# Padding every on-chip buffer of a three-block model kernel to begin at a multiple of 64 bytes

## The chip, the cores and the metric

The kernel runs on one core of one Trainium2 chip. The metric is the device time of that core in microseconds (us). Three runs of the kernel before gave 3527.54, 3527.82 and 3530.15 us, so the median is 3527.82 us.

## What is computed

The reference takes one sequence of 512 tokens of 1024 features through three blocks, all in 32-bit floats. Cut to what matters, a block is a few large matrix products between small stages:

```python
def first_block(x, ...):
    x = layer_norm(ALPHA * x + 0.5 * swiglu(x, w_gate, w_up, w_down), ...)   # 1024 -> 2816 -> 1024
    x = layer_norm(ALPHA * x + hybrid_mixer(x, w_in, ...), ...)   # attention and a state-space branch
    return layer_norm(ALPHA * x + 0.5 * swiglu(x, ...), ...)
```

The second block has another mixer (three branches) and a convolutional feed-forward of width 2816; the third has three branches (sparse attention, pooling, delta rule) and a feed-forward of width 4096. Every `x @ w` above is a product of 512 tokens with a weight matrix that is read from HBM once.

## The kernel before, in words

**The products.** TensorE multiplies in a reduced form of 32-bit float (`float32r`). To keep accuracy, each operand is split into a high and a low half, and each product is made of three matmuls: high with low, low with high, high with high. A weight unit of 128 partitions by 1024 floats lands by DMA in one of four buffers `ring` (line 413). ScalarE writes its high half into a buffer `w_high` (line 429), VectorE writes the rest into `w_low` (line 441). Each of the two has three buffers; some stages lend further pairs, named `f1d_place`, `o_place` and so on (`Down.place`, line 763).

**Three helpers issue nearly all large matmuls.** `tile_steps` (line 465) streams 512 tokens of the activations (`x_high`, `x_low`, or a branch's `..._yh`, `..._yl`) past 128x128 weights: 24 matmuls make one tile of 128 output features. `tensor_rows` (lines 735 to 737) and `tensor_down_tile` (lines 849 to 851) do the reverse: the weights are streamed, 512 floats wide, past 128x128 pieces of the activations (`x_high`, or small buffers `f1d_in`, `c2d_in`, `f3d_in`, `o_in`). In the trace a matmul is named `bank<-moving,stationary`: the first name is the operand that is streamed, the second the one that is loaded. Line 644 holds matmuls of 256 columns of a Strassen-like stage. The small stages use plain float32 matmuls.

**Order.** Every engine has its own hand-written program, tied by semaphores. Nothing in these programs reads an address: a buffer's place in memory sets no count, no order and no wait.

**Where buffers lie.** `Area.take` (line 151) hands out on-chip memory one buffer after the other. `self.at` counts floats per partition; the byte address is `ORIGIN + 4 * self.at`, and ORIGIN, 16512, is 258 times 64. At most FLOATS = 53200 floats are to be had. The first area (lines 232 to 246) holds what lives all through; every stage opens an area of its own behind it, at `b.base.at` or at a place inside an earlier stage. The places that follow from the sizes in the code, in floats, with what is left over when divided by 16 (16 floats are 64 bytes):

```
buffer                                     first float   over 16   bytes past a multiple of 64 / of 16
ring (4), const                            0 to 4608     0         0  / 0
cols (462 floats)                          4608          0         0  / 0
X, x_high, x_low, w_high (3), w_low (3)    5070 ...      14        56 / 8
hid, f1d_in, f2d_in, c2d_in, f3d_in        23830 ...     6         24 / 8
first block:  a_yh, a_yl (attention)       40160, 44256  0         0  / 0
first block:  z_yh, z_yl; o_in, o_place    28022 ...     6         24 / 8
second block: a_yh, g_yh, l_yh and lows    48918 ...     6         24 / 8
second block: o_place                      41756 ...     12        48 / 0
third block:  a_yh, a_yl (attention)       43068, 45116  12        48 / 0
third block:  p_yh, d_yh and lows; o_place 38950 ...     6         24 / 8
the last float taken by any buffer         53190
```

Three sizes cause it: `cols` has 462 floats (14 over 16), `cond` has 8, and in single stages 257x2, 514, 516 and 62 floats throw what follows off by another amount (and in the attention of the first block back on a multiple of 64 bytes, by five buffers of 514).

Of the kernel before, what the change touches and what calls it, by code (L numbers as in the profile page):

```python
# [16 lines left out]
FIRST = 4  # L17
ORIGIN = 16512
FLOATS = 53200
ALPHA = 2.0 ** 0.25  # L20
NEG = -1.0e30

# [122 lines left out]
class Area:  # L145
# [5 lines left out]
    def take(self, name, *shape, dtype=F32):  # L151
        n = 1
        for s in shape:
            n *= s
        assert self.at + n <= FLOATS, (name, self.at + n)
        self.b.n_tensors += 1
        t = self.b.nc.alloc_sbuf_tensor_at(f"{name}_{self.b.n_tensors}", [128, n], dtype,
                                           offset=ORIGIN + 4 * self.at, align_bytes=4)
        self.at += n
        a = t[:, :]  # L160
        if len(shape) == 2:
            return a.rearrange("p (a b) -> p a b", a=shape[0])
        if len(shape) == 3:
            return a.rearrange("p (a b c) -> p a b c", a=shape[0], b=shape[1])
        if len(shape) == 4:
            return a.rearrange("p (a b c d) -> p a b c d", a=shape[0], b=shape[1], c=shape[2])
        return a
# [1067 lines left out]
def gpsimd_ffn(b, s, ready):  # L1235
# [4 lines left out]
    for t in range(4):  # L1240
        for r in ready(t):
            gp.wait_ge(*r)
        gp.tensor_scalar(b.X[:, t, :], b.X[:, t, :], ALPHA, None, MUL).then_inc(*g.pool.up("alpha", t))

# [376 lines left out]
def gpsimd_qkv1(b, s):  # L1621
# [6 lines left out]
    for t in range(4):  # L1628
        gp.tensor_scalar(b.X[:, t, :], b.X[:, t, :], ALPHA, None, MUL).then_inc(*s.gw.pool.up("alpha", t))
    gp.wait_ge(*s.gw.pool.at("alpha", 3))  # L1630
# [3640 lines left out]
```

## Time and profile before

| | |
|---|---|
| median of three runs | 3527.82 us (3527.54 to 3530.15) |
| span of the profiled execution | 3528.6 us, clock 0.998 |
| TensorE (PE) busy | 3464.7 us, 98% |
| weight loads (PEld) | 2856.9 us, 81%, beside the matmuls |
| VectorE (DVE) | 2107.9 us, 60% |
| ScalarE (ACT) | 1497.4 us, 42% |
| GpSimd (POOL) | 333.9 us, 9% |
| DMA | 386.3 MB, 109 GB/s on average |

The profiled execution is one of its own; the page gives its span, 3528.6 us, and no other time for it. A matmul's duration in the trace is from its start to the modelled end of its results, and the next one starts long before that: durations overlap. What a matmul takes out of the span is the distance from its start to the start of the next, called its pitch here. It is read from the timeline view, where a group of equal matmuls in a row stands as one line with its count.

### The profile page before, as it was taken

How to read it: one execution, taken by the hardware profiler on the slowest of the kernel's cores; microseconds unless marked ns; L12 is line 12 of the kernel's file. 1: busy time of each engine (PE TensorE's matmuls, PEld its weight loads, DVE VectorE, ACT ScalarE, POOL GpSimd, SP SyncE). 2: the span in 40 equal slices, each digit the busy share in tenths (PEclk: the TensorE clock that was granted, in tenths of full speed). 3: DMA queues.
4: the chain of work that ended last, by engine and by line, in shares of the span. 5: the costliest groups of instructions: out<-in, count | busy, mean ns of one | idle time of the engine just before them, and what ended most of it. 6: DMA issues, size and time to landing. Idle time of an engine off the chain costs nothing. (4 is left out here: it accounts for less than half of the span.)

```text
span 3528.6 us, 45725 instructions
## 1 busy us (share of the span) xinstructions
PE 3464.7 (98%) x17532; PEld 2856.9 (81%) x17532; DVE 2107.9 (60%) x3344; ACT 1497.4 (42%) x2717; POOL 333.9 (9%) x374
## 2 busy tenths in 40 slices
PE   8999999999999999999999999999999999999999
PEld 7887888886777899887887788887787788888887
DVE  5456565678446787763344576667476567672256
ACT  2225344345443355536223363346254243452354
POOL 1000200003000100023000100000000104222100
PEclk9999999999999999999999999999999999999999
DMA  6556421220224334620322243245411320143365
GB/s 235 182 186 202 145 70 54 84 84 25 90 91 154 112 105 144 197 77 18 104 78 90 66 132 96 96 150 167 124 37 31 108 92 27 39 135 100 99 195 161
DMA packets 107974, 386.30 MB, mean 109 GB/s; under 512 B 12060, under 2 KB 14764, under 8 KB 107504
## 3 DMA queue, kind: packets, MB, share of 16 engines
q1 hardware_dynamic: 101088, 364.86, 32.0%
q0 software_dynamic: 4528, 16.43, 1.5%
q8 instruction: 142, 2.33, 0.3%
q10 hardware_dynamic: 2144, 2.10, 0.2%
q14 instruction: 72, 0.59, 0.1%
HBM read 379.13 MB, written 4.21 MB: 109 GB/s over the span
## 5 line engine op out<-in xcount | busy, mean ns | idle before, releaser
L441 DVE TENSOR_TENSOR w_low<-ring,w_high 128x1024 fp32r<-128x1024 f32 (+2 forms) x519 | 651.2, 1256 | 732.4 <-ACT w_high L429 724.5
L465 PE MATMUL bank<-x_low,w_high 128*128 128x512 f32 (+1 forms) x2144 | 839.6, 395 | 16.1 <-DVE w_low L441 9.8
L465 PE MATMUL bank<-x_high,w_low 128*128 128x512 f32 (+1 forms) x2144 | 826.6, 389 | 0.0
L429 ACT ACTIVATE w_high<-ring 128x1024 fp32r<-128x1024 f32 (+2 forms) x519 | 538.7, 1039 | 620.1 <-PE bank L465 257.5
L465 PE MATMUL bank<-x_high,w_high 128*128 128x512 f32 (+1 forms) x2144 | 542.8, 390 | 0.0
L465 PEld LDWEIGHTS bank<-x_low,w_high 128*128 128x128 f32 x2144 | 405.4, 189 | 104.6 <-issue 16.0
L465 PEld LDWEIGHTS bank<-x_high,w_low 128*128 128x128 f32 x2144 | 406.2, 189 | 84.8 <-issue 3.6
L465 PEld LDWEIGHTS bank<-x_high,w_high 128*128 128x128 f32 x2144 | 391.6, 190 | 87.8 <-issue 4.8
L735 PE MATMUL bank<-w_low,x_high 128*128 128x512 f32 (+1 forms) x384 | 147.0, 383 | 1.4 <-ACT z_z L2074 1.3
L737 PE MATMUL bank<-w_high,x_high 128*128 128x512 f32 (+1 forms) x384 | 145.6, 379 | 0.0
L736 PE MATMUL bank<-w_high,x_low 128*128 128x512 f32 (+1 forms) x384 | 145.5, 379 | 0.0
L735 PEld LDWEIGHTS bank<-w_low,x_high 128*128 128x128 f32 x384 | 72.3, 188 | 19.3 <-ACT z_z L2074 2.2
L736 PEld LDWEIGHTS bank<-w_high,x_low 128*128 128x128 f32 x384 | 72.3, 188 | 14.2 <-issue 0.2
L737 PEld LDWEIGHTS bank<-w_high,x_high 128*128 128x128 f32 x384 | 72.1, 188 | 14.3
L400 POOL DMA_DIRECT2D const<-in_consts x3 | 1.8, 588 | 862.6 <-DVE x_low L918 374.9
L3059 ACT ACTIVATE c_in<-bank 128x512 f32<-128x512 f32 x44 | 26.3, 598 | 108.6 <-PE bank L465 108.5
L4332 ACT ACTIVATE f_relu<-bank 128x512 f32<-128x512 f32 x32 | 19.2, 599 | 121.4 <-PE bank L465 121.4
L3082 DVE SCALAR_TENSOR_TENSOR c_y<-c_in,cols,c_y 128x512 f32<-128x512 f32 x88 | 66.2, 752 | 3.1
L849 PE MATMUL bank<-w_low,c2d_in 128*128 128x512 f32 x168 | 67.6, 403 | 0.0
L851 PE MATMUL bank<-w_high,c2d_in 128*128 128x512 f32 x168 | 67.4, 401 | 0.0
L850 PE MATMUL bank<-w_high,c2d_in 128*128 128x512 f32 x168 | 67.4, 401 | 0.0
L963 DVE SCALAR_TENSOR_TENSOR f_ada<-ring,cond,f_ada 128x512 f32<-128x512 f32 x84 | 65.0, 774 | 2.8
(746 smaller groups left out, 6963.9 us busy)
## 6 DMA issues: line engine op xcount, KB each, us to landing
ring<-in_W SPq DMA_DIRECT2D x686, 512.0 KB, 3.6
X<-in_x POOLq DMA_DIRECT2D x1, 2048.0 KB, 9.6
x_spill<-X POOLq DMA_DIRECT2D x1, 2048.0 KB, 8.1
X<-x_spill POOLq DMA_DIRECT2D x4, 512.0 KB, 3.6
ring<-in_W SPq DMA_DIRECT2D x4, 432.0 KB, 3.1
out<-X SPq DMA_DIRECT2D x3, 512.0 KB, 5.6
const<-in_consts POOLq DMA_DIRECT2D x1, 1133.0 KB, 11.6
f_hid<-in_xT ACTq DMA_DIRECT2D x4, 256.0 KB, 8.1
```

The source lines that it names most:

```text
L429: ac.activation(b.UH[u.place][:, 0:u.K * u.n], u.src(), ACT.Copy).then_inc(*b.split.act.up("high", i))
L441: dv.tensor_tensor(b.UL[u.place][:, 0:n], u.src(), b.UH[u.place][:, 0:n].bitcast(F32), SUB).then_inc(*b.split.dve.up("low", i))
L465: i = pe.matmul(out, w[:, k, c], v, start=n == 0 and q == 0, stop=last and q == 3 * K - 1)
L735: pe.matmul(out, xh, wl[:, q, :], start=k + q == 0, stop=False)
L736: pe.matmul(out, xl, wh[:, q, :], start=False, stop=False)
L737: i = pe.matmul(out, xh, wh[:, q, :], start=False, stop=k + q == 7)
L849: pe.matmul(out, u[:, 0, s], wl[:, 0, c], start=k == 0, stop=False)
L850: pe.matmul(out, u[:, 1, s], wh[:, 0, c], start=False, stop=False)
L851: x = pe.matmul(out, u[:, 0, s], wh[:, 0, c], start=False, stop=k == d.nk - 1)
L963: x = dv.scalar_tensor_tensor(acc, w[:, k, :], b.cond[:, 2 * q + k:2 * q + k + 1], acc, MUL, ADD)
L3059: ac.activation(s.cb[m % 3][:, 2:514], b.bk["c2u", m], ACT.Copy).then_inc(*g.act.up("copied", m))
L3082: dv.scalar_tensor_tensor(y, x[:, q:q + 512], b.col("ffn_conv_w_2", 44 * q + c), y, MUL, ADD).then_inc(*(g.dve.up("conv", m) if q == 2 els ...
```

## The change

`Area.take` rounds its position up to the next multiple of 16 floats before it places a buffer. The buffer's size, shape and content stay as they are; only first addresses move.

```diff
+LINE = 16
...
     def take(self, name, *shape, dtype=F32):
         n = 1
         for s in shape:
             n *= s
+        self.at += -self.at % LINE
         assert self.at + n <= FLOATS, (name, self.at + n)
```

The largest area ends at float 53190 before. Its padding adds 10 (2 behind `cols`, 8 behind `cond`), which makes 53200, the limit itself.

## Rows read from the trace of the kernel before

**Rows 1.** The page: busy time by engine.
```profile
PE 3464.7 (98%) x17532; PEld 2856.9 (81%) x17532; DVE 2107.9 (60%) x3344; ACT 1497.4 (42%) x2717; POOL 333.9 (9%) x374
```

**Rows 2.** Groups by form on PE (count, busy us, mean ns); lines 849 and 644 in whole.
```profile
L465 PE MATMUL bank<-x_low,w_high 128*128 128x512 f32 x1912 | 777.0, 406 | 2.0 <-issue 1.0 <-DVE w_low L441 0.7 <-DVE a_v L3398 0.2
...
L735 PE MATMUL bank<-w_low,x_high 128*128 128x512 f32 x320 | 127.8, 399 | 1.4 <-ACT z_z L2074 1.3
...
L465 PE MATMUL bank<-z_yl,w_high 128*128 128x512 f32 x128 | 52.0, 406 | 0.0
...
L465 PE MATMUL bank<-g_yl,w_high 128*128 128x512 f32 x32 | 12.7, 396 | 0.0
...
0.00:3529.00 3529.00, 390.72 (x976) 1.00 0.34 109
...
0.00:3529.00 3529.00, 162.72 (x1344) 1.00 0.34 109
```

**Rows 3.** Timeline, PE, a tile with x moving: start us, duration us, form, count.
```profile
206.95 0.39 PE L465 MATMUL bank<-x_low,w_high 128*128 128x512 f32 x1
...
212.57 0.39 PE L465 MATMUL bank<-x_low,w_high 128*128 128x512 f32 x1
```

**Rows 4.** Timeline, PE, second block, half a tile with g_y moving.
```profile
1811.13 0.40 PE L465 MATMUL bank<-g_yl,w_high 128*128 128x512 f32 x1
...
1813.95 0.39 PE L465 MATMUL bank<-g_yl,w_high 128*128 128x512 f32 x1
```

**Rows 5.** Timeline, PE, first block, a tile with a_y moving.
```profile
601.06 0.39 PE L465 MATMUL bank<-a_yl,w_high 128*128 128x512 f32 x1
...
606.63 0.39 PE L465 MATMUL bank<-a_yl,w_high 128*128 128x512 f32 x1
```

**Rows 6.** Timeline, PE, third block, half a tile with a_y moving.
```profile
2713.91 0.39 PE L465 MATMUL bank<-a_yl,w_high 128*128 128x512 f32 x1
...
2716.67 0.39 PE L465 MATMUL bank<-a_yl,w_high 128*128 128x512 f32 x1
```

**Rows 7.** Timeline, PE, a tile with z_y moving, in four pieces of 128.
```profile
1023.49 0.41 PE L465 MATMUL bank<-z_yl,w_high 128*128 128x512 f32 x1
...
1029.34 0.41 PE L465 MATMUL bank<-z_yl,w_high 128*128 128x512 f32 x1
```

**Rows 8.** Timeline, PE, 256 columns, x moving, o_place loaded: first, then second block.
```profile
1151.91 0.29 PE L465 MATMUL bank<-x_low,o_place 128*128 128x256 f32 x1
...
1154.80 0.29 PE L465 MATMUL bank<-x_low,o_place 128*128 128x256 f32 x1
...
2077.62 0.28 PE L465 MATMUL bank<-x_low,o_place 128*128 128x256 f32 x1
...
2080.50 0.29 PE L465 MATMUL bank<-x_low,w_high 128*128 128x256 f32 x1
```

**Rows 9.** Timeline, PE, o_place moving: first block to 1119.29, then second block.
```profile
1117.18 0.39 PE L849 MATMUL bank<-o_place,o_in 128*128 128x512 f32 x1
...
1119.29 0.40 PE L849 MATMUL bank<-w_low,o_in 128*128 128x512 f32 x1
...
2074.82 0.40 PE L849 MATMUL bank<-o_place,o_in 128*128 128x512 f32 x1
```

**Rows 10.** Windows, PE: length, busy (count), clock, DMA share, GB/s; c2d, then f3d.
```profile
2350.00:2410.00 60.00, 60.00 (x252) 1.00 0.57 183
...
3380.00:3500.00 120.00, 120.00 (x517) 1.00 0.61 188
```

**Rows 11.** Splits into o_place, windows 1100:1146 (first pair), 2040:2066 (second pair).
```profile
L441 DVE TENSOR_TENSOR o_place<-ring,o_place 128x1024 fp32r<-128x1024 f32 x9 | 11.0, 1222 | 1.4 <-ACT o_place L429 1.3
...
L429 ACT ACTIVATE o_place<-ring 128x1024 fp32r<-128x1024 f32 x9 | 9.4, 1046 | 0.4 <-DMA ring<-in_W 0.4
...
L441 DVE TENSOR_TENSOR o_place<-ring,o_place 128x1024 fp32r<-128x1024 f32 x6 | 7.3, 1223 | 1.1 <-ACT o_place L429 1.0
...
L429 ACT ACTIVATE o_place<-ring 128x1024 fp32r<-128x1024 f32 x6 | 6.3, 1046 | 0.0
```

## The prediction

> **What bounds the kernel now.** I read the page first: TensorE is busy 98% of the span and no other engine reaches two thirds [rows 1]. VectorE's, ScalarE's and the DMAs' work is hidden wherever TensorE streams, so a buffer's place can buy or cost time only through the matmuls themselves. The groups by form come next [rows 2]. The most frequent form streams 512 columns of x past weights: three groups of 1,912 (low with high, high with low, high with high), 5,736 matmuls. Weights streamed past x: 3 x 320 = 960. Line 849 has 976 and lines 850 and 851 the same, 2,928 in all. The streams of branch outputs follow: z_y 3 x 128 = 384; g_y, l_y, p_y, d_y and the second block's a_y 3 x 32 each, 480. With the 288 of the two other a_y these are 10,776 matmuls of 512 columns; at some 234 ns each they are 2,520 us, 71% of the span.
>
> The third view is the timeline, for the pitch, the distance from one start to the next. A tile with x moving begins at 206.95 and the next at 212.57: 5.62 us for 24 matmuls, 234.2 ns [rows 3]. Half a tile of g_y takes 2.82 us for 12, 235.0 ns [rows 4].  Here x lies 8 bytes past a multiple of 16 bytes, and so does g_y. Now the two operands that don't: the a_y of the first block begins at a multiple of 64 bytes, and its tile takes 5.57 us for 24, 232.1 ns [rows 5]; the a_y of the third block begins 48 bytes past one, which is a multiple of 16, and takes 2.76 us for 12, 230.0 ns [rows 6]. All four are loaded from the same w buffers, run through the same helper; the granted clock is 1.00 in the windows read, which is the 2.4 GHz level [rows 10]. The only thing I know that sets them apart is the first address of the moving operand. z_y is streamed as four pieces of 128, each of them 8 bytes off, and takes 5.85 us for 24, 243.8 ns [rows 7]: about 10 ns more for three more pieces, some 3 ns a piece, of the same size as the 2 to 4 ns between the one-piece cases.
>
> The loaded operand doesn't show this. 256 columns of x stream past o_place, which in the first block lies 8 bytes off 16 and in the second lies on a multiple of 16: 2.89 us for 24 (120.4 ns) against 2.88 us (120.0 ns) [rows 8]. So I put the gain to the moving operand's address, not to the loaded one's.
>
> **The change, part by part.** It adds and removes no instruction, wait or transfer. What moves is addresses. `ring` and `const` stay (they are at multiples of 64 bytes already); X, x, w and nearly every stage buffer go from 8 bytes past a 16-byte boundary to a multiple of 64. The class each stream lands in is that of rows 5, so I price with 232.1 and keep 230.0 as the good end and no gain as the bad end.
>
> - x streamed past w: 234.2 - 232.1 = 2.1 ns [rows 3, 5], times 5,736: 12.0 us. Ends: 0 and 4.2 x 5,736 = 24.1 us.
> - The 480 branch streams at 8 bytes off: 235.0 - 232.1 = 2.9 ns [rows 4, 5]: 1.4 us. Ends 0 and 5.0 x 480 = 2.4.
> - z_y, 384: nothing to 243.8 - 232.1 = 11.7 ns; whether a change of piece costs time for itself no row tells, so I take the middle, 5.9 ns: 2.3 us. Ends 0 and 5.3 (at 230.0).
> - Weights streamed past x, 960: no aligned case. Ends 0 and 4 ns; I take 1.0 ns, half of x's, because streams of weights show less in rows 9: 1.0 us, ends 0 and 3.8.
> - Weights streamed past small buffers, 2,928. o_place moving takes 2.11 us for 9 (234.4 ns) in the first block and 2.80 us for 12 (from 2074.82 to 2077.62 of rows 8; 233.3 ns) in the second, where it lies on 16 bytes [rows 8, 9]: 1.1 ns. The third block's f3d stretch has 120.00 us for 515 starts (two of the 517 were under way at the edges), 233.0 ns [rows 10], w's and places mixed. I take 1.1 ns for the third of them that stream from lent places (some 1,070) and nothing for w: 1.2 us. Ends 0 and 3 x 2,928 = 8.8.
> - 256 columns: 1,344 on line 644 [rows 2] and some 1,300 on line 465. One piece each, so the same absolute price is possible, but no aligned moving case exists. Between 0 and 2.1 ns, I take half: 1.0 x 2,640 = 2.6 us; good end 4 x 2,640 = 10.6.
> - Plain float32 matmuls, transposes: stay; their small stages wait on VectorE and ScalarE.
> - ScalarE and VectorE: writing into o_place takes ScalarE 1046 ns at either alignment and VectorE 1222 against 1223 ns [rows 11]. Nothing. The cover is TensorE's tile of 5.6 us over 2.3 us of splitting; if it fell away, an unchanged duration would still cost nothing.
> - DMA: the weights' ring doesn't move. The two 2 MB transfers of X and the spills do, outside TensorE's path.
>
> Sum: 12.0 + 1.4 + 2.3 + 1.0 + 1.2 + 2.6 = 20.5 us. From the profiled span, 3528.6 us, that is 3508.1; the median of the runs stands 0.8 below the span, so 3507.3, and I say 3507. A measurement of this kernel can tell about 0.2%, 7 us, from no change. With all good ends (24.1 + 2.4 + 5.3 + 3.8 + 8.8 + 10.6 = 55) it would be 3473.
>
> A page bears on the size. The Trainium skill, "SBUF — State Buffer", section "SBUF: two separate sides", says that on-chip memory is read in lines of 16 bytes and that a stream pays for each line it crosses into. A run of 512 floats that starts 8 bytes off touches 129 lines instead of 128; an estimate from that page is 234 / 129 = 1.8 ns, and by it the x term would be 10 us. Rows 3 and 5 agree with it.
>
> **The rivals.**
>
> *No change that can be told (25%).* What matters may be how moving and loaded operand lie to each other. x and w are both 14 over 16 floats, both 0 afterwards: their difference stays zero. In rows 5 and 6 the difference isn't a multiple of 16 bytes, and that alone could give 232.1 and 230.0. Against it stand rows 8, where the difference changes from one to the other kind and the pitch doesn't. Then x keeps 234.2, and the a_y of first and third block, which lose their odd difference, pay back 2.1 x 192 + 4.2 x 96 = 0.8 us; z_y may give 2. Time: 3526, between 3521 and 3534. The Trainium skill, "TensorE: Matmul & The Clock Gate", section "Back-to-back issue gap", is on this side: its gap for 512 columns is a function of columns and clock alone, 215.8 ns, with no address in it; the trace does not agree with its number (234.2 in rows 3), and its silence on addresses would mean 3528.
>
> *Slower (15%).* The stretch of c2d, weights streamed past c2d_in, has 60.00 us for 250 starts, 240.0 ns, where the same helper with the same alignments past f3d_in has 233.0 [rows 10]. Something in the addresses or in the phase of two streams locks c2d into a pattern that is 7 ns worse, and the same could catch other stages once everything lies at the same place within 64 bytes. Its place is any long stretch of equal matmuls; its price is about 6 ns each. It decides when more than 7 us / 6 ns = 1,170 matmuls beyond the gain are caught: with 20.5 us gained, 4,600 of them. If half of the 10,776 are caught and nothing is gained, 5,388 x 6 = 32 us: 3560. If x alone is, 3562. For it: the lock is there in the trace, unexplained. Against it: the x stream, the longest of all, shows no such pitch in rows 3.
>
> *A larger gain (12%).* The pitch goes to 230.0 or below everywhere, and c2d leaves its 240: 3473 by the good ends, with c2d's some 500 matmuls 3 us more. For it: rows 6. Against it: the operand of rows 5 is the one at a multiple of 64.
>
> That the padding doesn't take place is excluded by the arithmetic: X goes from float 5070 to 5072. It also just fits, 53190 + 10 = 53200.
>
> **How the numbers follow.** The forecast has 48%, no change 25%, slower 15%, the larger gain 12%. Faster by over 0.2%: 48 + 12 = 60%. The range reaches from 3480, which leaves out the best part of the larger gain, to 3535, which takes in all of no change and the mild part of slower; some 2 in 10 lie outside. The forecast's own range is 3495 to 3518.
>
> **What would show it.** In the changed kernel's timeline a tile of x should take 5.57 us (232.1 ns) instead of 5.62; z_y's 5.85 should fall to about 5.7; a_y of the first block should stay at 5.57; durations on ScalarE and VectorE should stay within 5 ns; TensorE's idle time should not grow. I am wrong if x stays at 234 (the rival on relative place), if a_y of the first block rises (its loaded operand's move matters), or if a stretch stands at 240.0 that did not before.

## The result and the profile after

The changed kernel takes 3469.49 us in the median of four runs (3467.41 to 3474.49), against 3528.45 us for the kernel before beside it (3527.54 to 3530.15): a ratio of 0.9835, 95% interval 0.9821 to 0.9849. It is faster by 59 us. The forecast was 3507 us with a range from 3480 to 3535: the sign was right and the size far off, on the side of the larger gain.

The page of the changed kernel, span and busy time by engine, which answers to [rows 1]:

```profile
span 3466.8 us, 45725 instructions
PE 3399.0 (98%) x17532; PEld 2838.3 (82%) x17532; DVE 2104.5 (61%) x3344; ACT 1495.5 (43%) x2717; POOL 336.3 (10%) x374
```

TensorE is busy 65.7 us less (3464.7 before), with the same 17,532 matmuls. The span falls by 61.8 us; TensorE's idle time grows from 63.9 to 67.8 us. VectorE and ScalarE stay within 4 us. So the whole difference lies in the matmuls' pitch, where the prediction had looked for it.

The timeline of the changed kernel, TensorE: a tile of x past w (to compare with [rows 3]), then a tile of a_y of the first block ([rows 5]); start, duration, form, count:

```profile
200.75 0.39 PE L467 MATMUL bank<-x_low,w_high 128*128 128x512 f32 x1
...
206.19 0.39 PE L467 MATMUL bank<-x_low,w_high 128*128 128x512 f32 x1
...
593.13 0.40 PE L467 MATMUL bank<-a_yl,w_high 128*128 128x512 f32 x1
...
598.72 0.39 PE L467 MATMUL bank<-a_yl,w_high 128*128 128x512 f32 x1
```

x takes 5.44 us for 24, 226.7 ns, where it took 5.62 us (234.2 ns). That is already below the 230.0 ns which the prediction held for the best case. a_y, at a multiple of 64 bytes before and after, takes 5.59 us (232.9 ns) against 5.57: almost the same.

A window in the middle of a long stretch of equal matmuls says the same with one line. Its columns are: window, length, TensorE's busy time, matmuls touched by it, clock, DMA share, GB/s. Two matmuls are cut by the edges, so the pitch is the length divided by the count less 2. One matmul more or less in the count is 0.4 ns in 120 us, 0.7 in 80 and 1.3 in 40, so smaller differences between windows say nothing. Four stretches of the kernel before, in this order: x past w, w past x, z_y past w, w past c2d_in:

```profile
2130.00:2250.00 120.00, 120.00 (x514) 1.00 0.29 92
1734.00:1774.00 40.00, 40.00 (x173) 1.00 0.38 119
1009.00:1089.00 80.00, 80.00 (x330) 1.00 0.37 118
2334.00:2414.00 80.00, 80.00 (x336) 1.00 0.60 192
```

The same stretches of the changed kernel, and last f3d_in, which answers to the second line of [rows 10]:

```profile
2130.00:2250.00 120.00, 120.00 (x531) 1.00 0.29 97
1702.00:1742.00 40.00, 40.00 (x178) 1.00 0.37 119
991.00:1071.00 80.00, 80.00 (x344) 1.00 0.36 118
2288.00:2368.00 80.00, 80.00 (x345) 1.00 0.60 197
3317.00:3437.00 120.00, 120.00 (x521) 1.00 0.62 191
```

Worked out: x past w from 234.4 to 226.8 ns, w past x from 233.9 to 227.3, z_y from 243.9 to 233.9, c2d from 239.5 to 233.2. The f3d stretch, w and lent places mixed, goes from 233.0 only to 231.2. Times their counts: 7.6 x 5,736 = 43.6 us, 6.6 x 960 = 6.3, 10.0 x 384 = 3.8, 6.3 x 504 = 3.2, in sum 57 of the 65.7 us. These products give all matmuls of a pair the pitch of one undisturbed stretch, so they are upper figures: added up from start to start over the two traces, waits included, x past w takes 34.9 us less, w past x 4.6, z_y 4.1 and c2d 2.6. The rest is in smaller groups. One is the stage of 256 columns (12 matmuls between the two lines), another the lent places past f1d_in (48 between the two lines). The timeline of the kernel before:

```profile
1267.48 0.65 PE L644 MATMUL bank<-f2s_sh,w_high 128*128 128x256 f32 x4
1268.93 0.65 PE L644 MATMUL bank<-f2s_sh,w_high 128*128 128x256 f32 x4
...
299.64 0.39 PE L849 MATMUL bank<-f1d_place,f1d_in 128*128 128x512 f32 x1
...
310.86 0.42 PE L849 MATMUL bank<-w_low,f1d_in 128*128 128x512 f32 x1
```

and of the changed kernel:

```profile
1262.70 0.63 PE L646 MATMUL bank<-f2s_sh,w_high 128*128 128x256 f32 x4
1264.11 0.63 PE L646 MATMUL bank<-f2s_sh,w_high 128*128 128x256 f32 x4
...
310.20 0.39 PE L851 MATMUL bank<-f1d_place,f1d_in 128*128 128x512 f32 x1
...
321.10 0.39 PE L851 MATMUL bank<-w_low,f1d_in 128*128 128x512 f32 x1
```

120.8 ns became 117.5, and 233.8 became 227.1.

What needs a cause is that buffers all at multiples of 64 bytes now run at four different pitches (226.8, 229.2, 232.9 and 233.9 ns). The table gives the first bytes modulo 256, from the sizes in the code, and the pitch of the pair. "Distance" is the loaded buffer's place less the moving one's, modulo 256. The pitches of g_y and of the two f3d rows are read like those of f1d_place, start to start over 24 to 48 equal matmuls.

```
moving     loaded      before: places, distance, ns      after: places, distance, ns
x          w           184, 184     0    234.4           192, 192     0    226.8
w          x           184, 184     0    233.9           192, 192     0    227.3
f1d_place  f1d_in      216, 216     0    233.8             0,   0     0    227.1
f3d_place  f3d_in      216, 216     0    233.7             0,   0     0    227.6
g_y (2nd)  w           216, 184   224    234.8             0, 192   192    229.2
a_y (1st)  w             0, 184   184    232.1            64, 192   128    232.9
z_y (1st)  w            88, 184    96    243.9           128, 192    64    233.9
w          c2d_in      184, 216    32    239.5           192,   0    64    233.2
w          f3d_in      184, 216    32    232.2           192,   0    64    233.3
```

The last two rows warn that the places modulo 256 are not the whole story: before the change w past c2d_in ran at 239.5 ns and w past f3d_in at 232.2, at the same places. No run here says why.

There were two ideas to test: that the start of each buffer counts (modulo 16, 32 or 64 bytes, of one operand or of both), and that the distance of the two operands counts.

### The profile page after: what moved, and what is told of

Same layout as the page of the kernel before. It is cut to its first block and busy times, and to the rows that moved or that the text cites. A ratio compares the mean times of both kernels' runs of the same rounds, so it can differ in the third digit from the quotient of the medians.

```text
span 3466.8 us, 45725 instructions
## 1 busy us (share of the span) xinstructions
PE 3399.0 (98%) x17532; PEld 2838.3 (82%) x17532; DVE 2104.5 (61%) x3344; ACT 1495.5 (43%) x2717; POOL 336.3 (10%) x374
## 5 line engine op out<-in xcount | busy, mean ns | idle before, releaser
L467 PE MATMUL bank<-x_low,w_high 128*128 128x512 f32 (+1 forms) x2144 | 828.6, 390 | 17.7 <-DVE w_low L443 11.1
L467 PE MATMUL bank<-x_high,w_low 128*128 128x512 f32 (+1 forms) x2144 | 814.9, 384 | 0.0
L467 PE MATMUL bank<-x_high,w_high 128*128 128x512 f32 (+1 forms) x2144 | 528.7, 384 | 0.0
```

The source lines that it names most:

```text
L467: i = pe.matmul(out, w[:, k, c], v, start=n == 0 and q == 0, stop=last and q == 3 * K - 1)
```

## Experiments

The times of the kernel before, beside each group of four runs, were 3529.97, 3529.68 and 3528.91 us. The lines in the fences of this section are windows on TensorE as above, 2130 to 2250 us for x past w.

### Start or distance: everything 8 bytes later

```diff
-ORIGIN = 16512
+ORIGIN = 16520
```

> Every buffer of the changed kernel 8 bytes later, so that none begins at a multiple of 16 bytes, with all distances between buffers as in the changed kernel. Theory A (where a buffer begins counts by itself): the matmuls of x past w go back from 226.7 ns to about 234 ns apart, and the time to about 3528 us. Theory B (only the distance between the moving and the loaded operand counts): they stay at 226.7 ns and the time at 3469 us. A time in between would say that both count.

Measured: 3511.78 us, ratio 0.9949 (0.9934 to 0.9963).

```profile
2130.00:2250.00 120.00, 120.00 (x519) 1.00 0.29 94
2321.00:2401.00 80.00, 80.00 (x349) 1.00 0.64 198
```

x past w is at 120 / 517 = 232.1 ns instead of 226.8: with every distance untouched, the start alone costs 42 of the 59 us. But it isn't 234.4 either: x was 56 bytes past a multiple of 64 before and is 8 past here, at distance 0 both times, so a start off the grid does not cost the same everywhere. It need not cost at all: c2d is faster here than in the changed kernel (230.5 against 233.2 ns). The expectation took a time in between for a sign that the distance counts too. This run can't show that, because it changes no distance.

### Which buffers: x and w, or the stages

x and w at their old places, the stages at the new ones:

```diff
-        self.at += -self.at % LINE
+        if self.at >= 23830:
+            self.at += -self.at % LINE
```

> x and w where they were before the change (8 bytes past a multiple of 16), every stage buffer as in the changed kernel. Theory A: x past w at 234 ns, 5,736 x 7.2 ns = 41 us slower than the changed kernel, and w past x, z_y past w and d_y past w back with it: 3515 to 3520 us. Theory B: x past w keeps its distance of 0 and so 226.7 ns; only the pairs of w with stage buffers move, 3470 to 3485 us. Theory C (the gain is in the stage buffers): under 3480 us.

Measured: 3507.96 us, ratio 0.9939 (0.9925 to 0.9954). The window of x, and 583 to 623 us, a_y of the first block:

```profile
2130.00:2250.00 120.00, 120.00 (x514) 1.00 0.29 95
583.00:623.00 40.00, 40.00 (x179) 1.00 0.32 104
```

x past w is back at 234.4 ns. That is the pitch of Theory A; the time is 7 us under its 3515. z_y, which the theory sent back with x, stays at 80 / 342 = 233.9 ns (1004 to 1084 us). a_y has 40 / 177 = 226.0 ns, faster than in either kernel: it lies at a multiple of 64 bytes, its w does not, and their distance is 120 instead of 128. l_y of the second block has the same places, 64 and 184; a tile of it, 24 matmuls between these lines, takes 5.44 us, 226.7 ns, where the changed kernel takes 5.61 us (from 1980.67 to 1986.28), 233.8 ns:

```profile
2002.76 0.39 PE L468 MATMUL bank<-l_yl,w_high 128*128 128x512 f32 x1
...
2008.20 0.39 PE L468 MATMUL bank<-l_yl,w_high 128*128 128x512 f32 x1
```

So a pair with one operand off the grid can be as fast as any, and a pair with both on it can be 7 ns slower.

The mirror image, x and w new, the stages at their old places:

```diff
-        self.at += -self.at % LINE
+        if name in ("X", "x_high", "x_low", "w_high", "w_low"):
+            self.at += -self.at % LINE
...
-        self.small = a.take("small", 256)
+        self.small = a.take("small", 254)
```

> x and w as in the changed kernel, every stage buffer where it was before the change. Theory A: x past w at 226.7 ns, so 3478 to 3487 us; the matmuls of the stage's own buffers back at 234 ns. Theory B, by which the old places of x and w were as good: about 3520 us. Theory C: about 3525 us.

Measured: 3481.85 us, ratio 0.9867 (0.9852 to 0.9882). Windows of x, of z_y and of a_y of the first block:

```profile
2130.00:2250.00 120.00, 120.00 (x532) 1.00 0.29 97
993.00:1073.00 80.00, 80.00 (x330) 1.00 0.37 118
577.00:617.00 40.00, 40.00 (x176) 1.00 0.33 100
```

x past w keeps 226.4 ns; z_y is back at 243.9. a_y, at its old place with w at the new one (distance 192), has 40 / 174 = 229.9. The two halves give 48.1 us and 22.0 us, together 70, where the change gives 59: they aren't independent, since w is an operand of nearly every stage's matmuls too.

### Which operand: x alone, or w alone

x 8 bytes off, w on the grid:

```diff
-        self.at += -self.at % LINE
+        if self.at >= 23830:
+            self.at += -self.at % LINE
...
+        a.at += 2
         self.UH = [a.take("w_high", SLOT, dtype=F32R) for _ in range(NU)]
...
-        self.small = a.take("small", 256)
+        self.small = a.take("small", 254)
```

> Of the changed kernel, only x is put back to 8 bytes past a multiple of 16 (it stands 8 bytes nearer to the buffers before it); w and the stage buffers stay at multiples of 64. Theory M (what counts of the two operands is the start of the moving one): x past w at 232 to 234 ns, 5,736 x 6 ns = 34 us above the changed kernel, about 3503 us, and w past x stays at 227 ns. Theory P (both must be aligned): x past w and w past x both at 231 to 234 ns, about 3508 us. Theory D (only the distance of the two matters, now 8 bytes): the same as P here, so the w past x matmuls tell M from P and D.

Measured: 3501.34 us, ratio 0.9917 (0.9902 to 0.9932). Windows of x past w, and 1716 to 1754 us, w past x:

```profile
2130.00:2250.00 120.00, 120.00 (x519) 1.00 0.30 97
1716.00:1754.00 38.00, 38.00 (x164) 1.00 0.40 122
```

w 8 bytes off, x on the grid:

```diff
-        self.at += -self.at % LINE
+        if self.at >= 23830 or name in ("X", "x_high", "x_low"):
+            self.at += -self.at % LINE
...
+        a.at += 126
         self.UH = [a.take("w_high", SLOT, dtype=F32R) for _ in range(NU)]
...
-        self.small = a.take("small", 256)
+        self.small = a.take("small", 128)
```

> Of the changed kernel, only w is put back to 8 bytes past a multiple of 16 (504 bytes further on, so 8 bytes short of its distance modulo 512); x and the stage buffers stay at multiples of 64. Theory M: x past w stays at 227 ns, w past x and w past the stage inputs go to 231 to 234 ns, 960 x 6 ns = 6 us and no more: 3472 to 3480 us. Theory P: x past w at 231 to 234 ns as well, 3500 to 3510 us.

Measured: 3501.69 us, ratio 0.9918 (0.9903 to 0.9933). The same two stretches:

```profile
2130.00:2250.00 120.00, 120.00 (x516) 1.00 0.29 92
1713.00:1751.00 38.00, 38.00 (x166) 1.00 0.40 125
```

Moving x off: 232.1 ns for x past w and 234.6 for w past x. Moving w off: 233.5 and 231.7. Each is slow in both roles. Theory M, the reading of the prediction by which only the moving operand's start counts, falls: an aligned x past a w that is off runs at 233.5 ns. What these two kernels can't separate is the start from the distance, which is 8 bytes in either; the run with everything 8 bytes later (distance 0, 232.1 ns) had shown that the start alone is enough to lose the gain.

### How fine the grid is: 32 and 16 bytes

```diff
-ORIGIN = 16512
+ORIGIN = 16544
```

> Every buffer of the changed kernel 32 bytes later: multiples of 32 and not of 64, all distances as in the changed kernel. Theory 64 (a start at a multiple of 64 is needed): x past w at 231 to 234 ns, about 3500 us. Theory 32 or 16 (the lines that count are shorter): 227 ns, 3469 us.

```diff
-ORIGIN = 16512
+ORIGIN = 16528
```

> Every buffer of the changed kernel 16 bytes later: multiples of 16 and not of 32, all distances as in the changed kernel. Theory 16 (a start at a multiple of 16 bytes is enough): x past w at 227.5 ns and 3469 to 3472 us, as with 32 bytes. Theory 32: x past w at 231 to 234 ns, 3495 to 3512 us, as with 8 bytes.

Measured: 3471.41 us for 32 bytes (0.9831, 0.9815 to 0.9848) and 3493.72 us for 16 (0.9907, 0.9891 to 0.9924). The windows of x, of the first and of the second kernel:

```profile
2130.00:2250.00 120.00, 120.00 (x531) 1.00 0.30 97
```

```profile
2130.00:2250.00 120.00, 120.00 (x523) 1.00 0.29 94
```

226.8 ns against 120 / 521 = 230.3, between the ranges of the two theories on 16 bytes. For x past w, at distance 0, a multiple of 16 bytes brings only a part of the gain; of 32, all of it. The 64 of the change are more than this pair needs. At another distance 16 bytes past the grid is the better start: z_y, at distance 64, has 80 / 349 = 229.2 ns in the second kernel and 233.9 in the changed one:

```profile
1002.00:1082.00 80.00, 80.00 (x351) 1.00 0.38 122
```

### The distance of the two operands

The six w buffers each at another distance from x; all at multiples of 64 bytes:

```diff
-        self.UH = [a.take("w_high", SLOT, dtype=F32R) for _ in range(NU)]
-        self.UL = [a.take("w_low", SLOT, dtype=F32R) for _ in range(NU)]
+        pads = iter((16, 16, 32, 16, 16, 16))
+
+        def unit(name):
+            a.at += next(pads)
+            return a.take(name, SLOT, dtype=F32R)
+
+        self.UH = [unit("w_high") for _ in range(NU)]
+        self.UL = [unit("w_low") for _ in range(NU)]
...
-        self.small = a.take("small", 256)
+        self.small = a.take("small", 144)
```

> All buffers at multiples of 64 bytes, but the six w buffers 64, 128, 256, 320, 384 and 448 bytes further (modulo 512) from x than in the changed kernel, where the distance is a multiple of 1024. Theory A (multiples of 64 bytes suffice): x past w stays at 226.7 ns in all six, 3469 us. Theory D (aligned buffers gain fully only if the moving and the loaded operand also stand at the same place modulo 256 or 512 bytes): x past w at 229 to 234 ns in at least four of the six, those at 256 telling whether the modulus is 256 or 512, and 3490 to 3510 us.

Measured: 3491.1 us, ratio 0.9892 (0.9875 to 0.9908). The last eight matmuls of a tile load from w_high alone. The timeline, three tiles one after the other, each by the start of those eight and of the next tile:

```profile
155.85 2.02 PE L473 MATMUL bank<-x_high,w_high 128*128 128x512 f32 x8
157.72 0.39 PE L473 MATMUL bank<-x_low,w_high 128*128 128x512 f32 x1
...
161.43 2.02 PE L473 MATMUL bank<-x_high,w_high 128*128 128x512 f32 x8
163.29 0.39 PE L473 MATMUL bank<-x_low,w_high 128*128 128x512 f32 x1
...
166.97 1.98 PE L473 MATMUL bank<-x_high,w_high 128*128 128x512 f32 x8
168.79 0.40 PE L473 MATMUL bank<-x_low,w_high 128*128 128x512 f32 x1
```

1.87, 1.86 and 1.82 us for eight: 233.8, 232.5 and 227.5 ns. The pattern comes back every three tiles, as the three buffers do. The trace doesn't number the buffers; in the order of their use the distances are 64, 128 and 256 bytes. With all starts on the grid and nothing but the distance changed, 22 us of the gain are gone. That multiples of 64 suffice falls.

That 256 is as good as 0 was then asked by itself, with w moved by 256 bytes against everything:

```diff
+        a.at += 64
         self.UH = [a.take("w_high", SLOT, dtype=F32R) for _ in range(NU)]
...
-        self.small = a.take("small", 256)
+        self.small = a.take("small", 192)
```

> The changed kernel with only w moved, by 256 bytes: its distance to x and to every stage buffer changes by 256. Theory modulus 256: every pitch stays, x past w at 227.5 ns and w past c2d_in at 233.3 ns, 3469 us. Theory modulus 512 or more: x past w at 229 to 233 ns, 3480 to 3500 us.

Measured: 3469.45 us, ratio 0.9828 (0.9813 to 0.9842).

```profile
2130.00:2250.00 120.00, 120.00 (x532) 1.00 0.30 97
2288.00:2368.00 80.00, 80.00 (x344) 1.00 0.61 198
```

226.4 ns for x and 233.9 for c2d, as in the changed kernel. For these pairs the distance counts modulo 256.

### A better layout

x and w together moved on by 320 bytes, so that w stands at 0 modulo 256, as the inputs of the down projections do:

```diff
+        a.at += 80
         self.X = a.take("X", 4, 1024)
...
-        self.small = a.take("small", 256)
+        self.small = a.take("small", 176)
```

> The changed kernel with x and w, both with the same distance between them, moved on by 320 bytes: they then begin at 256 modulo 1024, as the inputs of the down projections and of the attention's second block do (f1d_in, f2d_in, c2d_in, f3d_in, a_y and g_y of the second block), and no longer at the place of d_y and o_in of the third block. Theory D (distance 0 modulo 256 between moving and loaded gains what is left): w past c2d_in, f1d_in, f2d_in and f3d_in from 233.3 to 227 ns, 1,400 matmuls x 6 ns = 8 us; o_in and d_y of the third block back to 232 ns, 2 us lost: about 3463 us. Theory A (multiples of 64 suffice, the rest is scatter): 3469 us and 233 ns as before.

Measured: 3463.07 us (3461.49 to 3466.28), ratio 0.9811 (0.9796 to 0.9825). Windows of c2d_in and f3d_in:

```profile
2289.00:2369.00 80.00, 80.00 (x355) 1.00 0.62 198
3315.00:3435.00 120.00, 120.00 (x531) 1.00 0.63 192
```

c2d 226.6 ns (233.2 in the changed kernel) and f3d 226.8 (231.2). One number of padding gives 6 us more, as expected.

Then the same place for y and for all inputs:

```diff
-        self.at += -self.at % LINE
+        at = 32 if name[-3:] in ("_yh", "_yl", "_in") else None
+        self.at += -self.at % LINE if at is None else (at - self.at) % 64
...
+        a.at += 80
         self.X = a.take("X", 4, 1024)
...
-        self.small = a.take("small", 256)
+        self.small = a.take("small", 176)
...
+        a.at += 32
         xs_at = a.at
```

> x and w moved on by 320 bytes, and all split inputs of the products (every buffer of y, high and low, and the inputs of the projections o and the down projections) put at the same place as w modulo 256; all else at multiples of 64. Theory D: against the run of x and w alone (3463 us) z_y from 232.4 to 227 ns (383 matmuls, 2 us), a_y of the first block and w past o_in to 227 ns (190 and 330 matmuls, 2.5 us), o_place past o_in to 227 ns (219, 1 us), the rest 1 us: 3456 us. Theory A (the distance matters for x and w only): 3463 us.

Measured: 3460.14 us (3456.72 to 3462.46), ratio 0.9802 (0.9788 to 0.9817). z_y is at 80 / 353 = 226.6 ns (233.9 in the changed kernel):

```profile
990.00:1070.00 80.00, 80.00 (x355) 1.00 0.38 125
```

(The last line of the diff moves the area on which z_y is laid.) The median fell by 3 us where 7 were expected, and the four runs of this kernel scatter over 6 us; the spans of the two profiled executions stand 6 us apart (3461.5 and 3455.5). So the pitch came as expected and the size of the gain is known to some 3 us only. One pair that the expectation counts wasn't put at distance 0: o_place of the second block lies 64 bytes past its o_in. In both kernels the 256-column matmuls lie at distance 0 and are slower than in the changed kernel (120.0 ns below, against 117.5). The next run differs by one line. (It also carries two lent places f2d_place and the units off distance 0 to f2d_in, which costs about 1 us there.)

```diff
-        at = 32 if name[-3:] in ("_yh", "_yl", "_in") else None
+        at = {"f2s_sh": 16, "f2s_sl": 16, "f2s_unit": 48}.get(name, 32 if name[-3:] in ("_yh", "_yl", "_in") else None)
```

> As the run before, and in the part of seven products with 256 columns the units 64 bytes past the place of x, and the two halves of its inputs 64 bytes short of the place of w, modulo 256: the kernels so far show 114 to 118 ns there for a matmul of 256 columns at such a distance and 120 ns at distance 0. Theory E (at 256 columns distance 0 is the slow one, 64 bytes is a fast one): 1,200 matmuls x 2 to 4 ns, 2 to 5 us under the run before, 3452 us. Otherwise: no difference.

Measured: 3450.75 us (3450.24 to 3451.74), ratio 0.9777 (0.9762 to 0.9791): 18.7 us, 0.54%, under the changed kernel, and the ranges of their runs don't overlap. The spans say that some 6 of the 9 us between the last two kernels are this line's (3455.5 and 3449.0); 768 such matmuls at 6.7 ns would be 5.1, the other 432 of the stage the rest. The timeline, 12 matmuls between two starts; first the run without the line:

```profile
1259.64 0.64 PE L648 MATMUL bank<-f2s_sh,w_high 128*128 128x256 f32 x4
1261.08 0.64 PE L648 MATMUL bank<-f2s_sh,w_high 128*128 128x256 f32 x4
```

and with it:

```profile
1256.68 0.62 PE L648 MATMUL bank<-f2s_sh,w_high 128*128 128x256 f32 x4
1258.04 0.62 PE L648 MATMUL bank<-f2s_sh,w_high 128*128 128x256 f32 x4
```

120.0 ns against 113.3. For this pair of 256 columns distance 0 is the slow one and 64 bytes the fast one, the other way round than at 512 columns. How fast 64 bytes are isn't settled by the places: x past f2s_unit stands at 192 and 0 in the changed kernel and in the kernel with w alone off the grid. A tile of 24 matmuls, first in the changed kernel (117.9 ns), then in the other (114.2):

```profile
1219.21 0.28 PE L646 MATMUL bank<-x_low,f2s_unit 128*128 128x256 f32 x1
...
1222.04 0.28 PE L646 MATMUL bank<-f2s_sl,w_high 128*128 128x256 f32 x1
...
1219.81 0.28 PE L648 MATMUL bank<-x_low,f2s_unit 128*128 128x256 f32 x1
...
1222.55 0.28 PE L648 MATMUL bank<-f2s_sl,w_high 128*128 128x256 f32 x1
```

Every tile of that stretch keeps to its kernel's value, at the same two places; why they differ is open.

All twelve runs and the two kernels (x past w by its window, time of the median):

```
kernel                                    us        x past w, ns
before                                    3528.45   234.4
everything 8 bytes later                  3511.78   232.1
x and w old, stages new                   3507.96   234.4
w 8 bytes off, x on the grid              3501.69   233.5
x 8 bytes off, w on the grid              3501.34   232.1
everything 16 bytes later                 3493.72   230.3
six distances                             3491.10   231.2
x and w new, stages old                   3481.85   226.4
everything 32 bytes later                 3471.41   226.8
the change                                3469.49   226.8
w 256 bytes further                       3469.45   226.4
x and w at 0 modulo 256                   3463.07   226.8
y and inputs too                          3460.14   226.4
and 256-column operands 64 bytes apart    3450.75   226.8
```

## Why the prediction was wrong in size

**What held.** That only the pitch can move the time: TensorE's busy time fell by 65.7 us with the same instructions, and its idle time changed by 4. That VectorE's and ScalarE's work costs the same at the new places. That the padding fits.

**What came true by luck.** a_y of the first block stayed (5.57 to 5.59 us), for the prediction because only the moving operand's place counts and a_y's was good already. But with the stages moved alone it ran at 226.0 ns, with x and w moved alone at 229.9, and with both at 232.9, against 232.1 before. Two moves that each make it faster together undo each other.

**The step that failed: the x term.** It was 2.1 ns x 5,736 = 12.0 us. Measured it is 7.6 ns x 5,736 = 43.6 us at the pitch of the long stretch and 34.9 us from start to start over the whole trace; 23 to 32 of the 38 us by which the forecast missed are here. The prediction priced the aligned case with the 232.1 ns of [rows 5], "the class each stream lands in". In those rows the moving operand is aligned and the loaded one, w, is 8 bytes off 16, and the two are 184 bytes apart. The pitch belongs to the two places together: the same half-aligned a_y ran at 226.0 ns once it stood 120 bytes from w, and x past w with w or x alone off the grid at 233.5 and 232.1. No row of the kernel before had both operands on the grid at distance 0, as the change puts x and w. (The clock was not in it: [rows 10] give it for c2d and f3d alone, but windows of x, z_y and a_y show 1.00 too.)

**Why the loaded operand was struck out.** From [rows 8], 120.4 against 120.0 ns for o_place at two alignments, the prediction concluded that the loaded operand's start doesn't matter. In both of those rows the moving x is 8 bytes off, and the distance changes along with the start. With x off, mending the other showed nothing here. The comparison varied one factor at a bad level of the other, and an effect of the two together can't be read so. The same holds for o_place moving in [rows 8, 9]: the o_in loaded beside it is 8 bytes off in both blocks.

**The good end was not an end.** 230.0 ns of [rows 6] was taken as the best that could come; it belongs to an operand at a multiple of 16 bytes and not of 32, past a misaligned w. The best measured is 226 to 227. So the larger gain, with 12%, was the nearest case, and that its 3473 lies close to the measured time is partly luck: x was priced short (4.2 ns instead of 7.6), and the pitch did not go to 230.0 or below everywhere (z_y 233.9, c2d 233.2, a_y 232.9).

**The rival on the relative place** was right in that the distance matters and wrong in what it made of it. Its sentence that x keeps 234.2 because its distance stays 0 fell with the first window: starts count at an unchanged distance. Neither decides before the other, as a_y at distance 120 showed. Evidence for it was in the text: z_y's 243.8 was put down to its four pieces (and half of it so in the sum), but when the place alone was changed it ran at 226.6, the pitch of x, in the same four pieces. Pieces cost nothing here. And c2d's 240, left unexplained, became 230.5, 233.2 or 226.6 when nothing but the layout changed. That was the lock of the slower rival, and here the change took it away. What it was stays open: at the same places modulo 256, w past f3d_in ran at 232.2 ns.

**The smaller terms.** w past x: 1.0 expected, 6.3 measured. z_y: 2.3 and 3.8 (both measured at the pitch of one stretch). The 256-column stage: 1.0 ns expected, 3.3 measured. Weights past small buffers: 1.2 expected; c2d alone gave 3.2, lent places past f1d_in 6.7 ns each. In the mixed f3d stretch, 1.8 ns better, the lent places fell from 233.7 to 227.6 ns and w rose from 232.2 to 233.3.

**The page's rule.** By the estimate from the Trainium skill ("SBUF — State Buffer", section "SBUF: two separate sides") a start off 16 bytes costs one more line, 1.8 ns. Its agreement with rows 3 and 5 was chance: x past w at distance 0 lost 5.3 ns by 8 bytes (232.1 against 226.8), and starts at multiples of 16 (230.3 ns) and of 32 (226.8 ns) cross no line more or less than each other, by that rule, and differ by 3.5 ns. The measurement decides.

## What to carry to other kernels

Where TensorE streams back to back, the addresses of the two operands are a cost. The layout that was fast for every pair of 512 columns that got it: both at multiples of 64 bytes (32 were enough for x past w) and at the same place modulo 256. Alignment alone left some pairs 7 ns slow, and at 256 columns the same place was the slow choice. Read it from a window in a pure stretch (length by count), pair by pair, before and after: a pitch that differs between pairs of the same shape may be a layout to be mended, and a run with other places tells. And when a trace is read for the price of one factor, look at what level the other one stood.

## What the runs showed of the hardware

- With the clock at 1.00 in every window quoted, the pitch of a 512-column float32r matmul with a full load beside it went from 226 to 243.9 ns with nothing but addresses changed, and of a 256-column one from 113.3 to 120.8.
- Starts, for x past w at distance 0: on a grid of 32 bytes 226.8 ns, 8 bytes past it 232.1, 16 past it 230.3, 24 past it 234.4. At distance 64 z_y had 233.9 on the grid and 229.2 at 16 bytes past it.
- Distance on the grid, 512 columns: 0 and 256 give 226.4 to 227.5 ns, 64 gives 233 to 234, 128 gives 232 to 233, 192 gives 229 to 230. At 256 columns, 0 gives 120.0, and 64 gives 113.3 to 117.9 in the stage of seven products, with two values at the same places.
- Off the grid the distances don't order so: a_y and l_y on the grid, 120 bytes from a w that is off it, ran at 226.0 and 226.7 ns; with w on it, at distance 128, at 232.9 and 233.8.
- Places modulo 256 are not enough: w past c2d_in 239.5 ns and w past f3d_in 232.2, both at 184 and 216.

That two streams, the moving operand's and the next weights', meet in the memory is a guess that no run here shows: the runs show addresses and pitches. Open too is why 256 columns want another distance, what a moving operand off the grid, past a loaded one on it, costs at distances other than 8 bytes, and what besides the places modulo 256 sets the pitch.
